# A two-block transformer kernel on one core: order of the first loads and products, of the factors at the post norm, and of the last quarter of X

## The reference

```python
for i in range(DEPTH):                      # first block, DEPTH = 2
    x = x + 0.5 * swiglu_ffn(rmsnorm(x, ffn1_norm[i]), ffn1_wi[i], ffn1_wo[i])
    ...                                     # mLSTM and window attention, gated, w_out
    x = x + 0.5 * swiglu_ffn(rmsnorm(x, ffn2_norm[i]), ffn2_wi[i], ffn2_wo[i])
    gate = jax.nn.sigmoid(rmsnorm(x, ple_norm[i]) @ w_ple_gate[i])
    x = x + gate * (p[i] @ w_ple[i])
# second block, twice: ffn, mixer (convolution, pooling, attention), ffn, and then
# x = rms_norm(x, post_norm_2[i]) over the whole row
def rmsnorm(x, g):
    xf = x.astype(jnp.float32)
    y = xf * lax.rsqrt(jnp.mean(xf * xf, axis=-1, keepdims=True) + EPS)
    return (y * g.astype(jnp.float32)).astype(x.dtype)
def swiglu_ffn(x, wi, wo):                  # hidden width 2816, the second block alike
    g, u = jnp.split(x @ wi, 2, axis=-1)
    return (jax.nn.silu(g) * u) @ wo
```

## Time and profile before

| | us |
|---|---|
| median of 3 runs | 2064.91 (2062.87 to 2065.75) |
| profiled execution, its own time | 2065.13 |
| its span, first to last instruction | 2063.3 |
| TensorE busy | 2042.8 (99%) |
| VectorE busy | 1499.9 (73%) |
| ScalarE busy | 1095.1 (53%) |
| GpSimd busy | 128.0 (6%) |
| data moved | 378.82 MB, mean 184 GB/s |

### The profile page before, as it was taken

The page is one execution under the profiler, slowest core; times in us unless marked ns, Lnnn a source line. Parts: engine busy times, 40 slices in busy tenths (PEclk is TensorE's granted clock), DMA queues, the critical chain, the costliest instruction groups (busy, mean ns, idle before and its releaser), DMA issues.

```text
span 2063.3 us, 27840 instructions
## 1 busy us (share of the span) xinstructions
PE 2042.8 (99%) x10800; PEld 1744.7 (85%) x10800; DVE 1499.9 (73%) x2261; ACT 1095.1 (53%) x1637; POOL 128.0 (6%) x140
## 2 busy tenths in 40 slices
PE   9999999999999999999999999999999999999998
PEld 7888888888888888888888888878888888878887
DVE  6776677777677767677767776897677777798766
ACT  5444665544554456655446444675445544675443
POOL 1000100000000001000001000150000000160000
PEclk9999999999999999999999999999999999999999
DMA  7654545555555555455555655436555655435553
GB/s 250 204 184 162 197 153 198 185 184 190 192 185 185 194 165 173 165 194 189 189 192 189 235 193 191 168 115 195 194 191 184 204 185 193 169 107 195 193 193 124
DMA packets 105539, 378.82 MB, mean 184 GB/s; under 512 B 12173, under 2 KB 12837, under 8 KB 105152
## 3 DMA queue, kind: packets, MB, share of 16 engines
q1 hardware_dynamic: 102768, 368.95, 54.1%
q0 software_dynamic: 2208, 7.71, 1.3%
q10 hardware_dynamic: 432, 0.39, 0.1%
HBM read 375.73 MB, written 1.27 MB: 183 GB/s over the span
## 4 chain that ended last, share of the span: by engine, by line
PE 94%; DVE 4%; ACT 1%; DMA 1%; issue 0%; POOL 0%; POOLq 0%; DVEq 0%; ACTq 0%
PE pb L432 31%; PE pb L437 16%; PE pb L360 13%; PE pb L361 13%; PE pb L362 13%; DVE scr L1719 2%; PE pb L385 1%; PE pb L483 1%; PE pb L407 1%; PE pb L406 1%; PE pb L405 1%; DVE wlo L1705 1%; DVE scr L2384 0%; DMA raw<-in_W 0%; PE pb L908 0%
## 5 line engine op out<-in xcount | busy, mean ns | idle before, releaser
L1705 DVE TENSOR_TENSOR wlo<-raw,whi 128x1024 fp32r<-128x1024 f32 (+1 forms) x702 | 847.9, 1215 | 53.7 <-ACT whi L1085 53.2
L1085 ACT ACTIVATE whi<-raw 128x1024 fp32r<-128x1024 f32 (+1 forms) x706 | 730.6, 1045 | 289.1 <-PE pb L437 169.8
L432 PE MATMUL pb<-XT,whi 128*128 128x512 f32 x2816 | 703.1, 391 | 1.8 <-DVE XT L1719 1.3
L432 PEld LDWEIGHTS pb<-XT,whi 128*128 128x128 f32 x2816 | 515.5, 188 | 101.8 <-issue 1.8
L437 PEld LDWEIGHTS pb<-XT,wlo 128*128 128x128 f32 x2816 | 384.1, 190 | 27.5
L437 PE MATMUL pb<-XT,wlo 128*128 128x256 f32 x2816 | 392.6, 282 | 0.0
L1817 DVE TENSOR_REDUCE sbuf_s<-pb 128x256 f32<-128x512 f32 x240 | 154.4, 685 | 235.1 <-PE pb L437 235.1
L360 PE MATMUL pb<-whi,HTh 128*128 128x512 f32 x816 | 321.6, 394 | 0.0
L361 PE MATMUL pb<-wlo,HTh 128*128 128x512 f32 x816 | 319.6, 392 | 0.0
L362 PE MATMUL pb<-whi,HTl 128*128 128x512 f32 x816 | 317.7, 389 | 0.0
L1155 ACT ACTIVATE sbuf_s<-sbuf_s 128x256 f32<-128x256 f32 x120 | 49.7, 419 | 343.1 <-DVE sbuf_s L1824 343.0
(11 more groups left out here) (231 smaller groups left out, 1483.0 us busy)
## 6 DMA issues: line engine op xcount, KB each, us to landing
raw<-in_W SPq DMA_DIRECT2D x694, 512.0 KB, 4.2
raw<-in_W SPq DMA_DIRECT2D x8, 264.0 KB, 2.9
scr<-in_bc POOLq DMA_DIRECT2D x2, 640.0 KB, 5.8
raw<-in_W SPq DMA_DIRECT2D x4, 256.0 KB, 4.7
scr<-scratch POOLq DMA_DIRECT2D x8, 128.0 KB, 4.8
scr<-mrow POOLq DMA_DIRECT2D x2, 512.0 KB, 5.1
scr<-in_slope POOLq DMA_DIRECT2D x1, 1024.0 KB, 11.0
scr<-in_Pg POOLq DMA_DIRECT2D x1, 1024.0 KB, 14.2
```

The costliest lines, as they stand in the source:

```text
L432: pe.matmul(pb[b + j][:, :], h[:, k:k + P], xs, start=c == 0, stop=False)
L1085: return act.activation(o, i, ACT.Copy, scale=scale)
L1705: dve.tensor_tensor(wlo[u % W_SLOTS][:, 0:c], raw[u % RAW_SLOTS][:, 0:c], whi[u % W_SLOTS][:, 0:c].bitcast(F32), ALU.subtract).then_inc(*u ...
```

## The change

- SP's queue issues only X's first quarter, and then weights. X columns 256 to 511 are issued by ScalarE's queue between `ident` and `gcol`, columns 512 to 1023 behind `gcol`.
- The second warm-up has two products instead of five.
- In units 0 and 1 the high products wait for `hi` alone; the low products, which follow all high ones of the unit, wait for `lo`. The turns of chunks 2 and 3 stand behind chunk 0's products instead of chunk 1's. ScalarE and VectorE have their first operations in another order.
- At n = 11 `turn_r` stands between the high and the low products of unit 6 instead of ahead of it.
- At the end the last job is two: columns 512 to 767 go on in their bank, and the last six products for columns 768 to 1023 go into bank 4 from zero. VectorE adds bank 3 whole (with what columns 768 to 1023 have had so far), and bank 4's quarter on top. Squares are taken in five pieces, the sum of row block 1 in two steps. VectorE scales columns 0 to 767 of row block 1, ScalarE columns 768 to 1023, and the outputs are cut likewise.

```diff
-WARM_UP = (8, 5)
+WARM_UP = (8, 2)
+LAST_X = [(0, 0, 512), (0, 512, 1024), (1, 0, 512), (1, 512, 768), (1, 768, 1024)]
...
+                    if m == LAST and (n, t) == (1, 1):
+                        last_quarters(u, lh, ll, chunks, ready)
+                        continue
...
+            def last_quarters(u, lh, ll, chunks, ready):
+                fill(4)
+                for q in (2, 3):
+                    o, cut = pb[OB[1][1] if q == 2 else 4][:, 0:256], slice(256 * q, 256 * q + 256)
+                    for i, c in enumerate(chunks):
+                        ready(c, 1)
+                        h, l = whi[(u + i) % W_SLOTS][:, cut], wlo[(u + i) % W_SLOTS][:, cut]
+                        ah, al = lh[:, c, P:2 * P], ll[:, c, P:2 * P]
+                        pe.matmul(o, ah, h, start=q == 3 and i == 0, stop=False)
+                        pe.matmul(o, ah, l, start=False, stop=False)
+                        ins = pe.matmul(o, al, h, start=False, stop=i == 1)
+                        if q == 3:
+                            ins.then_inc(*up("used", u + i))
+                        elif i == 1:
+                            ins.then_inc(*up("used", u + 1, 3))
...
-                        if u < 2 and i == 2:
+                        if (u, i) in ((0, 1), (1, 2)):
                             for later in ((2, 3), (4, 5, 6, 7))[u]:
                                 turn_x(0, later)
-                        w.wait_ge(*(at("lo", u, "a") if u < 2 and i < 2 else at("lo", u)))
+                        if u < 2:
+                            w.wait_ge(*(at("hi", u, "a") if i < 2 else at("hi", u)))
+                        else:
+                            w.wait_ge(*at("lo", u))
...
+                    if between is not None:
+                        between()
                     for i in range(4):
                         c = 4 * half + i
+                        if u < 2:
+                            w.wait_ge(*(at("lo", u, "a") if i < 2 else at("lo", u)))
...
-                    if k == 6:
+                    if k == 6 and n != 11:
                         turn_r()
...
-                        gate_up(u, f, half)
+                        gate_up(u, f, half, turn_r if (n, k) == (11, 6) else None)
...
 (ScalarE)
             act.dma_start(ident[:, :], d["ident"]).then_inc(*landed("ident"))
+            act.dma_start(X[:, :, 256:512], d["x"][:, :, 256:512]).then_inc(*landed("xin1"))
             act.dma_start(gcol[:, :], d["gcol"]).then_inc(*landed("gcol"))
+            act.dma_start(X[:, :, 512:1024], d["x"][:, :, 512:1024]).then_inc(*landed("xin2"))
...
-            for c in range(4):
-                high_x(0, c)
-                split_half(c // 2, c % 2)
+            high_x(0, 0)
+            split_half(0, 0)
+            high_x(0, 1)
+            split_half(0, 1)
+            high_x(0, 2)
+            high_x(0, 3)
+            split_half(1, 0)
+            split_half(1, 1)
...
 (VectorE, at the end)
+                add(0, 0, 512)
+                gain(0, 0, 512)
+                add(0, 512, 1024)
+                gain(0, 512, 1024)
+                add(1, 0, 512)
+                mean_of(0, 0)
+                gain(1, 0, 512)
+                add(1, 512, 1024)
+                gain(1, 512, 768)
+                add(1, 768, 1024)
+                mean_of(1, 2)
...
                 dve.tensor_scalar(y[:, 0, :], y[:, 0, :], r_end[:, 0:1], None, ALU.mult).then_inc(*up("out_v", 0))
-                mean_of(1)
+                w.wait_ge(*at("ss", LAST, 1, 768))
+                w.wait_ge(*at("end_sum"))
+                dve.tensor_tensor(v_end[:, 1:2], v_end[:, 1:2], ends[:, 4:5], ALU.add).then_inc(*up("norm_v", LAST, 1))
+                gain(1, 768, 1024)
                 w.wait_ge(*at("post_r", LAST, 1))
...
+                dve.tensor_scalar(y[:, 1, 0:768], y[:, 1, 0:768], r_end[:, 1:2], None, ALU.mult).then_inc(*up("out_v", 1))
...
 (VectorE, at the start)
+            low_x(0, 0)
+            low_x(0, 1)
+            split_half(0, 0)
+            low_x(0, 2)
+            low_x(0, 3)
+            split_half(0, 1)
+            split_half(1, 0)
+            split_half(1, 1)
...
 (SP)
+            sp.dma_start(X[:, :, 0:256], d["x"][:, :, 0:256]).then_inc(*landed("xin0"))
             for u in range(2):
-                c = 256 * u
-                sp.dma_start(X[:, :, c:c + 256], d["x"][:, :, c:c + 256]).then_inc(*landed(f"xin{u}"))
                 for half in range(2):
...
-            sp.dma_start(X[:, :, 512:1024], d["x"][:, :, 512:1024]).then_inc(*landed("xin2"))
```

More of the change, by code:

```diff
@@ L412, in tail, with gate_up @@
                     empties[OB[t][n]] = ("x", m, t, n)
+            def last_quarters(u, lh, ll, chunks, ready):
[13 more added lines that the diff above has]
+                            ins.then_inc(*up("used", u + 1, 3))
             def ffn(s, n, m, u0):
-                def gate_up(u, f, half):
+                def gate_up(u, f, half, between=None):
                     b = 4 + 2 * (f % 2)
@@ L1680, in scalar @@
                     mixer2(s, layer, n, m, u0)
-            ends = col(3, "ss_end", 4)
-            for t in range(2):
-                for h in range(2):
-                    w.wait_ge(*at("x", LAST, t, h))
-                    w.wait_ge(*at("ss", *in_junk[-1]))
-                    in_junk.append((LAST, t, h))
-                    act.activation(junk[:, 0:512], X[:, t, h * 512:(h + 1) * 512], ACT.Square, scale=1.0 / 32.0,
-                                   accum_out=ends[:, 2 * t + h:2 * t + h + 1]).then_inc(*up("ss", LAST, t, h))
+            ends = col(3, "ss_end", 5)
+            for j, (t, a, z) in enumerate(LAST_X):
+                w.wait_ge(*at("x", LAST, t, a))
+                w.wait_ge(*at("ss", *in_junk[-1]))
+                in_junk.append((LAST, t, a))
+                act.activation(junk[:, 0:z - a], X[:, t, a:z], ACT.Square, scale=1.0 / 32.0,
+                               accum_out=ends[:, j:j + 1]).then_inc(*up("ss", LAST, t, a))
             r_end = col(3, "r_end", 2)
             w.wait_ge(*at("post_r", LAST, 1))
-            w.wait_ge(*at("x_gain", 1, 0))
-            copy(y[:, 1, 0:512], y[:, 1, 0:512], r_end[:, 1:2]).then_inc(*up("out_a"))
+            w.wait_ge(*at("x_gain", 1, 768))
+            copy(y[:, 1, 768:1024], y[:, 1, 768:1024], r_end[:, 1:2]).then_inc(*up("out_a"))
             w.wait_ge(*at("out_a"))
-            act.dma_start(out[P:2 * P, 0:512], y[:, 1, 0:512]).then_inc(*landed("out_last"))
+            act.dma_start(out[P:2 * P, 768:1024], y[:, 1, 768:1024]).then_inc(*landed("out_last"))
         def vector(dve, w):
@@ new lines, in last_into_x, with add @@
+                ends, v_end, r_end = col(3, "ss_end", 5), col(3, "v_end", 2), col(3, "r_end", 2)
+                def add(t, a, z):
+                    o = pb[4][:, 0:256] if a == 768 else pb[OB[t][a // 512]][:, :]
+                    if a == 768:
+                        w.wait_ge(*at("x", LAST, 1, 512))
+                    w.wait_ge(*(at("used", u) if a == 768 else at("used", u, 3 if a == 512 and t else 2 * (a // 512) + t)))
+                    axpy(X[:, t, a:z], o, factor[t], X[:, t, a:z], ALU.mult, ALU.add).then_inc(*up("x", LAST, t, a))
@@ new lines, in gain, with mean_of @@
+                def gain(t, a, z):
+                    w.wait_ge(*at("x", LAST, t, a))
+                    dve.tensor_tensor(y[:, t, a:z], X[:, t, a:z], post_gain[:, a:z], ALU.mult).then_inc(
+                        *up("x_gain", t, a))
+                def mean_of(t, j):
+                    w.wait_ge(*at("ss", LAST, t, 512))
+                    name, key = ("norm_v", (LAST, 0)) if t == 0 else ("end_sum", ())
+                    axpy(v_end[:, t:t + 1], ends[:, j:j + 1], EPS, ends[:, j + 1:j + 2], ALU.add, ALU.add).then_inc(
+                        *up(name, *key))
@@ L1781, in last_into_x @@
+                w.wait_ge(*at("bc2", 3))
+                add(0, 0, 512)
[9 more added lines that the diff above has]
+                mean_of(1, 2)
                 w.wait_ge(*at("post_r", LAST, 0))
-                for h in range(2):
-                    w.wait_ge(*at("x_gain", 0, h))
+                for a in (0, 512):
+                    w.wait_ge(*at("x_gain", 0, a))
@@ L2627, in mixer2 @@
                 into_x(u0 + 25, [1.0, 1.0], m)
-            for c in range(4):
-                low_x(0, c)
-                split_half(c // 2, c % 2)
+            low_x(0, 0)
[6 more added lines that the diff above has]
+            split_half(1, 1)
             split(2)
@@ L2864, in sync @@
             w.wait_ge(*at("out_v", 1))
-            sp.dma_start(out[P:2 * P, 512:1024], y[:, 1, 512:1024]).then_inc(*landed("out", 1))
+            sp.dma_start(out[P:2 * P, 0:768], y[:, 1, 0:768]).then_inc(*landed("out", 1))
             w.wait_ge(*at("out_last"))
```

23 lines of the change are left out of this document (2 added, 21 removed).

## The result

The changed kernel takes 2067.74 us (median of 20 runs, 2066.3 to 2069.91), the kernel before 2064.65 on the same chip (20 runs, one of them a stray of 8154.22). The ratio is 1.0017 [1.0011, 1.0023]: slower, by 3.1 us between the medians, where 2064.1 had been forecast. The profiled execution of after took 2067.88 us with a span of 2065.8; that of before 2065.13 and 2063.3, so the pair of traces holds a difference of 2.5 in the span (2.6 before rounding).

A forecast was written before the change was run, and what follows sets the result against it. TensorE's queue was taken to bound the kernel, matrix products being 94% of the span. From the profiled 2065.13, start -1.2, post norm -0.15 and end +0.5 gave 2064.3, as a median 2064.1; range 2062.1 to 2066.1 (8 in 10).

The forecast's parts named there:

- landing of gcol at 6.9: Start: gcol, behind X's second quarter on ScalarE's queue, lands at 6.9 us; bounds 5.6 and 8.0.
- three signs: Wrong if first product starts past 8.5, clock is below 1 in first 15 us, or stretch behind last product isn't longer.
- X0 near 5.6: Start: X's first quarter lands 0.3 to 0.4 us later, near 5.6, sharing the engines with X's second quarter.
- First product 7.95: Start: first wide product at 7.95 us, 0.25 us later than before.
- From there to unit 2 in 7.5 us: Start: measured durations summed through units 0 and 1, from the first product at 7.95 to 15.45.
- Unit 2 at 15.45, start -1.2: Start: TensorE ready for unit 2 at 15.45 instead of 16.66, a gain of 1.2 us.
- The cap that I set from unit 2's weights (-1.5): Start: unit 2's weights, assumed to land as before, limit the gain to 1.5 us.
- Post norm -0.15: Post norm near 1608 us: gain of 0.15 us, TensorE waiting 0.8 for VectorE's low part; bounds -0.95 and 0.
- End +0.5: End: 0.5 us slower, from VectorE's added operations behind the last product; bounds +0.2 and +0.9.
- Rivals 1 and 2: Start: gcol passes only at 8.0, total 2065.1, 15%; TensorE's clock falls to 1.2 GHz, total 2066.1, 15%.
- Rival 1: Start: gcol passes only at 8.0, 2065.1, 15%; against it, X0 and W0 would need SP's queue as slow.
- Rivals 3 and 4: Everything pays in full, sum -2.5, 2062.4, 12%; the end is a gain of 0.3, sum -1.65, 2063.3, 8%.

The follow-up runs named there:

- old end: The changed kernel with the end of the kernel before (four jobs of 512 columns, squares in four pieces): 2066.73 us, ratio 1.0015.
- long warm-up: The changed kernel with 12 products instead of 2 in the second warm-up: 2066.09 us, ratio 1.0011.
- last kernel of the third set: The changed kernel with X's second half on SP's queue behind unit 1's weights, X's second quarter still ahead of gcol: 2067.67 us, ratio 1.0016.
- gcol first and the old end: The changed kernel with gcol ahead of X's second quarter on ScalarE's queue and the end of the kernel before: 2063.65 us, ratio 0.9995.
- late split: The changed kernel with gcol ahead of X, VectorE's end reordered, and at n = 11 VectorE's weight split behind the gating products: 2062.41 us, ratio 0.9989.
- new end in its better order: The changed kernel with gcol ahead of X; VectorE adds both pieces first, last gain product beside GpSimd's power, last scaling as before: 2064.13 us, ratio 0.9996.

## Why the prediction was wrong

**The step that failed** is the landing of gcol at 6.9 in the part on arrivals, and with it the place of the clock's fall: a rival beside it instead of what follows from it. The landing rests on "The transfers do not get faster. Their rate is 389 GB/s from 4.8 us on, with the engines fully busy, so only their order changes." They got slower. With X's second quarter ahead of gcol in ScalarE's queue the engines are nearly as busy and move a little over half as much from 4 to 6 us. The lower rate shows in all four profiles of that order: 128 and 221 GB/s in after, 115 and 230 with the old end, 131 and 235 with the long warm-up, 127 and 218 in the last kernel of the third set. In the seven profiles with gcol first it is 190 to 250 and 277 to 324, and in the three with all of X on SP's queue 220 to 261 and 389 to 391.

That rate is only part of gcol's lateness. It landed at 7.99 instead of 6.9. The 0.24 MB that were missing at 7.2 us are 0.6 us at 389 GB/s (an estimate). Another 0.3 is the prediction's own step from the 7.2 of X's second quarter to 6.9, for which it gives no reason. What is left, 0.2, is not resolved; the even shares of the two queues, on which the landing rested too, aren't in the trace (97.0% against 12.6% of the engines' time from 3.5 to 4 us). And at the same low rate gcol landed at 7.17 with the old end, at 8.48 with the long warm-up and at 7.70 in the last kernel of the third set, so the rate doesn't fix its landing.

The measured 2067.74 lies outside the range of 2062.1 to 2066.1, though a change of 0.15% is still the "same" that had 93%. Of the three signs that the prediction named for being wrong two came: the first product past 8.5, and the clock below 1 in the first 15 us. The third, an end that isn't longer, did not.

Step by step:

- *X0 near 5.6.* It landed at 4.45 (0.75 + 3.7), earlier than before. The sharing with X's second quarter was paid by gcol and the weights instead.
- *First product 7.95.* It was 9.23, +1.28; 1.09 of that is gcol's landing.
- *From there to unit 2 in 7.5 us.* It took 8.74. With the clock kept it took 7.72 (long warm-up), so 1.0 is the clock and 0.2 the steps.
- *Unit 2 at 15.45, start -1.2.* It was 17.97. The prediction set its 15.45, a start of products, against the chain's 16.66; against the 16.49 of the timeline its gain would have been 1.04, and the measured shift is +1.5. In this execution another 0.5 was lost by unit 4, where the weights came late. With gcol first, unit 2 began at 14.59 to 15.13. The product order was costed well: alone it gave 1.05 us with all transfers as before. The cap that I set from unit 2's weights (-1.5) held with X on SP's queue, where ScalarE began on them at 12.58 and TensorE waited 0.58 us for VectorE's low part ahead of unit 2. With gcol first ScalarE began on them at 11.30, and unit 2 came 1.9 us earlier than before: there "I leave that" was wrong.
- *Post norm -0.15.* It was 0.0, with the idle time where it was forecast (1.06 instead of 0.8). The mechanism was right: VectorE's unbroken chain was the second bound, and only with that shortened too did the stage give 1.1 us.
- *End +0.5.* It was +0.5: the last issue +0.55, the tail +0.5. The additions ended where the prediction put them, 1.7 us behind the last product. The power took 0.67 instead of 0.55.
- *Sum.* Forecast for the span was -0.85; measured +2.6. Of the 3.4 between them 2.7 stood at unit 2 (0.2 of it the misread 16.66), 0.5 more by unit 4, 0.15 at the post norm; what is left lies below what two executions differ by.

**Rivals.** Rivals 1 and 2 both came true, and at the same time. I had priced them apart, gcol at 8.0 as +0.25 and a fall of the clock as +1.15, each on top of a forecast that had the other right. But the first prepares the second: gcol late makes TensorE idle for 2.3 us and more, and at the start the clock fell with each such idle time (2.30, 2.74, 3.45 us), while it stayed up with those of 0.2 to 1.5 (1.48 with gcol first and the old end). Added by my own prices they are -0.85 for the forecast's sum, +1.1 for gcol, +2.0 for the clock: +2.25. That this is close to the 2.6 measured is luck in part: the clock cost 1.0 and not 2.0, and the 0.5 by unit 4 and the misread 0.2 were in no price. The chance that I gave to that sum was nothing. Rival 1's "against" failed with the same step: the first weights on SP's queue took 7.1 instead of 4.7 us to landing, and only X0, ahead of it all, was not late. Rivals 3 and 4 did not occur.

The length of an idle time alone doesn't settle it. In the middle of the program TensorE stood idle for 2.2 us or more 15 times in the profiles kept, and the clock fell at 7 of them. The longest brought no fall ("late split" kernel, product and stretch behind it):

```profile
1374.31 1.53 PE L511 MATMUL pb<-ident,scr 128*128 128x128 f32 x12 [3.02 <-DVE scr L1753]
```

```profile
1374.30:1380.00 5.70, 5.69 (x42) 5.33 (x43) 5.54 (x18) 4.20 (x6) 0.87 (x1) 1.00 0.00 0
```

**What stays open.** Why the packets are slow when X's second quarter leads the second queue was not found. Packets of 1 KB took 0.10 us in the mean from 3.75 to 5.5 us, 0.046 undisturbed. The order isn't all that differs between the kernels: the packets of X's second quarter begin at 3.0 us in the four slow profiles, while those of its first quarter, from the same rows of X, still run on SP's queue (until 3.5 to 4.4), and at 4.2 to 4.8 in the seven with gcol first. Whether gcol's place or this overlap matters was not tested; other sizes or a small transfer between the two were not tried either. Nor is it known what made the clock fall behind one idle time in mid-program and not behind another of the same length. The difference of the medians, 3.1 us, is 0.35 above that of the two profiled executions (2067.88 and 2065.13); gcol's landing varies by over one us between executions, and one profile of each kernel doesn't show its middle. The Trainium skill, "DMA: Bandwidth & Descriptors", section "Issuing engines are not separate DMA queues", has a second issuing engine save only time of issuing. The kernels with gcol first agree as to gain: moving X's second half back to SP's queue changed nothing that could be measured. As to loss the measurement differs: with X's second quarter ahead of gcol the second queue cost 44% of the bytes from 4 to 6 us (349 GB/s summed over the two, against 624).

The fastest version against before is the one with gcol first, the turn inside and the late split: 0.9989 [0.9980, 0.9998] with the new end in its better order. With the old end it came to 0.9993 [0.9984, 1.0002], and to 0.9991 [0.9983, 1.0000] with X's second half on SP. The three were not compared closely enough to rank them; about 1.5 to 2.3 us are to be had.

## What to carry to other kernels

Ahead of the first product, ask for each queue which small transfer everything waits for, and keep it at the head: 56 KB of constants behind 256 KB of data cost 3 us here, first by waiting and then by the clock. Two rivals of which one prepares the other need a case of their own with both, not only a place side by side. Where two engines' chains meet a point close together, an edit to one of them moves the wait and gives nothing; look for what shortens the second by the same amount before either is tried alone.

## What the runs showed of the hardware

- The rate of 16 busy DMA engines isn't fixed by their being busy. With X's second quarter ahead of gcol in the second queue it was 115 to 131 GB/s from 4 to 5 us and 218 to 235 from 5 to 6; with gcol first 190 to 250 and 277 to 324; with X on one queue 220 to 261 and 389 to 391.
- TensorE's granted clock fell to 0.50 with idle times of 2.30, 2.74 and 3.45 us at the start: 0.6 us behind the end of the first two, and within the third. It stayed there for 3.4 us behind the first two and for 6.8 with the third, which cost 1.0 us in front (long warm-up against after) and 2.0. Single falls in mid-program (between 1375 and 1843 us) came in some profiles and not in others, at 7 of 15 idle times of 2.2 us or more and twice, near 1830, with none of that length; one costs some 1.5 to 1.7 us, which is as much as most of the differences sought here.
- The clock column shows 1.00 from the start of every profile, though the first 16 products took 236 ns each, as at 1.2 GHz. It can't be read ahead of the first change.
- A power of 128x1 on GpSimd took 0.55 us with no gain product beside it, and 0.67, 0.94 and 0.99 beside one of VectorE's. It ended 0.40 to 0.42 us behind that product's end each time.
